# The next layer's modulation in feed forward: weighted row sums on VectorE in place of products on TensorE

## The reference, cut to what matters

```python
silu_c = jax.nn.silu(c)
silu_cc = jax.nn.silu(c_ctx)
for l in range(DEPTH):
    mod = silu_c @ ada_w[l] + ada_b[l]
    modc = silu_cc @ ada_w[l] + ada_b[l]
    sh1, sc1, g1, sh2, sc2, g2 = [m[:, None, :] for m in jnp.split(mod, 6, axis=-1)]
    ...
    h = h + g1 * y
    h = h + g2 * swiglu(modulate(h, norm2_g[l], sh2, sc2), ffn_w_in[l], ffn_w_out[l])

def swiglu(h, w_in, w_out):
    g, u = jnp.split(h @ w_in, 2, axis=-1)
    return (jax.nn.silu(g) * u) @ w_out
```

## Time and profile before

| | |
|---|---|
| median of 3 runs | 4071.4 us (4070.13 to 4071.9) |
| span of the profiled execution | 4078.4 us |
| mean granted clock of TensorE | 0.952 |
| TensorE busy | 3830.4 us (94%) |
| VectorE busy | 1355.6 us (33%) |
| ScalarE busy | 1249.7 us (31%) |
| GpSimd busy | 1260.6 us (31%) |
| DMA | 342.84 MB, mean 84 GB/s |

### The profile page before, as it was taken

One profiled execution on the slowest core, in us unless ns is written; L12 is line 12 of the kernel. 1 busy time (PEld: TensorE's weight loads), 2 busy tenths in 40 slices (PEclk: granted clock), 3 DMA queues, 4 the chain that ended last, 5 costly groups with the idle time before them and its releaser, 6 DMA issues. The chain is left out here.

```text
span 4078.4 us, 77356 instructions
## 1 busy us (share of the span) xinstructions
PE 3830.4 (94%) x32782; PEld 3174.4 (78%) x32782; DVE 1355.6 (33%) x2689; ACT 1249.7 (31%) x2182; POOL 1260.6 (31%) x658
## 2 busy tenths in 40 slices
PE   6998999999999999989799999989999989989997
PEld 5877788888777677768698888768888868667785
DVE  3345211111444211166557765251111140543111
ACT  3234311112346322232234443232111142643222
POOL 2201222222334343432234432122322223634442
PEclk7999999999999999999879989999999989999998
DMA  4223232232200434333201100133233212012221
GB/s 174 68 97 108 88 119 87 102 110 88 79 5 32 155 134 164 131 111 110 83 21 30 28 22 24 63 119 108 73 119 110 71 52 73 20 45 88 94 88 71
DMA packets 119705, 342.84 MB, mean 84 GB/s; under 512 B 34687, under 2 KB 41343, under 8 KB 119039
## 3 DMA queue, kind: packets, MB, share of 16 engines
q1 hardware_dynamic: 119423, 338.75, 24.1%
HBM read 323.89 MB, written 16.93 MB: 84 GB/s over the span
## 5 line engine op out<-in xcount | busy, mean ns | idle before, releaser
L204 POOL TENSOR_TENSOR feed_low<-ring,feed_high 128x1024 fp32r<-128x1024 f32 (+1 forms) x236 | 620.5, 2629 | 1356.2 <-ACT feed_high L197 1324.2
L221 PE MATMUL ps<-hn_high,feed_high 128*128 128x512 f32 x2016 | 720.3, 357 | 9.3 <-DVE h L1204 5.1
L221 PE MATMUL ps<-hn_low,feed_high 128*128 128x512 f32 x2016 | 714.1, 354 | 0.0
L221 PE MATMUL ps<-hn_high,feed_low 128*128 128x512 f32 x2016 | 713.3, 354 | 0.0
L221 PEld LDWEIGHTS ps<-hn_high,feed_high 128*128 128x128 f32 x2016 | 381.2, 189 | 89.8 <-issue 24.6
L221 PEld LDWEIGHTS ps<-hn_high,feed_low 128*128 128x128 f32 x2016 | 381.0, 189 | 53.7
L221 PEld LDWEIGHTS ps<-hn_low,feed_high 128*128 128x128 f32 x2016 | 381.3, 189 | 51.5
L1379 DVE TENSOR_TENSOR ps<-feed_gate,ps 128x768 f32<-128x768 f32 (+1 forms) x88 | 73.0, 829 | 1004.4 <-PE ps L221 985.4
L197 ACT ACTIVATE feed_high<-ring 128x1024 fp32r<-128x1024 f32 (+1 forms) x240 | 272.7, 1138 | 369.5 <-PE ps L221 369.4
L221 PE MATMUL ps<-feed_hid_high,feed_high 128*128 128x512 f32 (+1 forms) x1056 | 380.2, 360 | 0.0
L221 PE MATMUL ps<-feed_hid_high,feed_low 128*128 128x512 f32 (+1 forms) x1056 | 376.8, 357 | 0.0
(11 more groups left out here) (592 smaller groups left out, 7491.9 us busy)
## 6 DMA issues: line engine op xcount, KB each, us to landing
feed_side_ring<-in_ada SPq DMA_DIRECT2D x144, 512.0 KB, 5.9
ring<-in_ffn_g SPq DMA_DIRECT2D x88, 512.0 KB, 3.5
ring<-in_ffn_u SPq DMA_DIRECT2D x88, 512.0 KB, 3.5
ring<-in_ffn_d SPq DMA_DIRECT2D x64, 704.0 KB, 4.1
diff_side_ring<-in_ada SPq DMA_DIRECT2D x32, 512.0 KB, 4.3
ring<-in_od_in SPq DMA_DIRECT2D x24, 512.0 KB, 3.4
ring<-in_ev_in SPq DMA_DIRECT2D x23, 512.0 KB, 4.4
ring<-in_even_in SPq DMA_DIRECT2D x20, 512.0 KB, 3.8
```

Source lines behind the costliest of these rows:

```text
L204: pool.tensor_tensor(self.low[:, j % self.slots, 0:w], feed.ring[:, slot, 0:w], self.high[:, j % self.slots, 0:w].bitcast(F32), ALU.subtra ...
L221: mm = pe.matmul(dst, weights[a], values[b], start=first and n == 0, stop=last and n == 2)
```

## The change

For the three feed forwards with side work, `SideSums` takes the place of `SideModulation`:

- VectorE reads the tiles of `ada` itself. For each block of 128 x 512 and each of the two vectors it multiplies by a scalar of its own for each partition and adds to a running sum: 16 instructions for a group (`weigh`), of which the first two only multiply. In "first" all four tiles stand behind the chunk, in "up" two tiles behind each chunk.
- TensorE sums over partitions: four products of 256 columns for a group, with a matrix of 32 columns of which the first is 1 (`add`), in the place where `turn` stood. `accumulate` is gone.
- VectorE transposes the sums in blocks of 32 x 32 and copies every 32nd column into PSUM (`take`), behind the first chunk of an iteration. `finish` now has 16 small additions instead of 2.
- `feed_side_ring` has three slots instead of four; the fourth tile of a group takes the slot of the first. A slot is freed by VectorE, not by TensorE.
- One small DMA at the head of each stage goes.

```diff
-        ("first", 1, [(s % SIDE, io[w], 0, 24 * h + s) for s in range(4)]),
-        ("up", HALF // 2, [(s % SIDE, io[w], 4, 24 * h + 4 + s) for s in range(4)]))]
+        ("first", 1, [(s % 3, io[w], 0, 24 * h + s) for s in range(4)]),
+        ("up", HALF // 2, [(s % 3, io[w], 4, 24 * h + 4 + s) for s in range(4)]))]
...
+class SideSums:
...
+    def weigh(self, dve, i, tiles):
+        side = self.k.side
+        for j in tiles:
+            slot, before, per = side.count(side.at, j)
+            dve.wait_ge(side.landed[slot], 16 * per * i + 16 * (before + 1))
+            for b in range(2):
+                c, weights = 2 * j + b, side.ring[:, slot, 512 * b:512 * b + 512]
+                for s in range(2):
+                    scalar = self.vec[:, c, s:s + 1]
+                    if c == 0:
+                        ins = dve.tensor_scalar(self.sums[:, s, :], weights, scalar, None, ALU.mult)
+                    else:
+                        ins = dve.scalar_tensor_tensor(out=self.sums[:, s, :], in0=weights, scalar=scalar, in1=self.sums[:, s, :],
+                                                       op0=ALU.mult, op1=ALU.add)
+                if b == 0:
+                    dve.drain()
+            ins.then_inc(side.used[slot], 1)
+            dve.drain()
+        if tiles[-1] == 3:
+            dve.sem_inc(self.summed, 1)
+
+    def add(self, pe, group):
+        pe.wait_ge(self.summed, group + 1)
+        if not (isinstance(group, int) and group == 0):
+            pe.wait_ge(self.acc_read, group)
+        for s in range(2):
+            for f in range(2):
+                q = 32 * (2 * s + f)
+                mm = pe.matmul(self.acc[q:q + 32, :], self.pick[:, :], self.sums[:, s, 256 * f:256 * f + 256], start=True, stop=True)
+        mm.then_inc(self.added, 1)
+
+    def take(self, dve, group):
+        dve.wait_ge(self.added, group + 1)
+        dve.transpose(self.turned[:, :], self.acc).then_inc(self.acc_read, 1)
+        dve.drain()
+        dve.tensor_copy(self.parts[:, bass.ds(8 * group, 8)], self.turned[:, :].rearrange("p (b w) -> p b w", w=32)[:, :, 0:1].rearrange("p b w -> p (b w)"))
+        dve.drain()
...
-                    if next_c and isinstance(i, int):
-                        sm.accumulate(pe, 0, 6 * h)
-                    elif next_c and p == 0:
-                        sm.turn(pe, i + 6 * h)
-                    elif next_c:
-                        sm.accumulate(pe, i, i + (6 * h + 1))
+                    if next_c and p == 0 and not isinstance(i, int):
+                        sm.add(pe, i + 6 * h)
...
                 chunk(0, 0, 0, e)
                 if next_c:
-                    sm.copy(dve, 0, 6 * h)
+                    sm.weigh(dve, 0, range(4))
                 if h == 0 and norm.kept:
                     norm.keep(dve)
                 feed.at, side.at = up, side_base + 2 * h + 1
                 with dve.Fori(0, HALF // 2) as i:
                     for p in range(2):
                         chunk(i, p, 2 * i + (p + 1), e1)
-                    if next_c:
-                        sm.copy(dve, i, i + (6 * h + 1))
+                        if next_c and p == 0:
+                            sm.take(dve, i + 6 * h)
+                        if next_c:
+                            sm.weigh(dve, i, range(2 * p, 2 * p + 2))
```

## The result

The changed kernel takes **4124.0 us** (median of 4 runs, 4119.9 to 4127.6), the kernel before beside it 4071.7 (4070.1 to 4074.9): ratio 1.0119, 95% interval 1.0100 to 1.0138. It is slower by 52 us; 4106 (4050 to 4155) was forecast.

A forecast was written before the change was run, and what follows sets the result against it. TensorE, busy 94%, was taken as the bound. Terms of +57.0 us at 512 tokens, -31.8 and +4.5 at 768, and +5 for `finish` gave +34.7 on 4071.4: 4106 us, range 4050 to 4155.

The forecast's parts named there:

- TensorE, -2.32 us for a group: Side work of 2.87 us a group gives way to 0.55 us of `add`; over 36 groups -83.5 us if nothing else waits.
- VectorE's weighings: A group's 16 instructions take 0.46 us for the first two and 0.73 for the other 14: 11.1 us, plus GpSimd collisions.
- The first chunk of a half: VectorE weighs all four tiles there, delaying the next multiplication; at 512 tokens the second iteration starts 7.5 us later.
- The chain at 512 tokens: From slot 0's release through the `ring` tile's issue, landing, rounding and subtracting to TensorE's start: a 4.75 us pause each iteration.
- The step "0.53 us later": Within the 512-token chain, SyncE issues the next iteration's first `ring` tile 0.53 us after the fourth side tile.
- The clock, 1.7 us for a pause: TensorE's clock falling around each 512-token pause costs 1.7 us more, making an iteration 29.0 us, +4.2 us.
- 768 tokens: The same chain stays hidden by 0.45 us, an iteration gains 2.3 us; -10.6 us a half, three times -31.8.
- `keep`: In the third feed forward's first half, its 9.05 + 6.29 us follow the weighings; second iteration 12.7 us later, half +4.5 us.
- `finish`: At a stage's end, 16 instructions of 0.16 us each replace two; the stage ends 1.7 us later, three times, 5 us.
- A: Rival: the saving comes through, the side slot holding `ring` back less; complete 3993 us, in part 4060 us; chance 0.18.
- B: Rival: a wash, the two halves of the sum cancelling within 8 us, 4071 us; chance 0.09.
- C: Rival: VectorE becomes the bound through GpSimd collisions, waits and drains; +40, 4146 us; chance 0.2, within slower.

The follow-up runs named there:

- experiment 2: Changed kernel with the fourth side tile issued behind the next iteration's four `ring` tiles and 14 of a group's 16 weighings left out: 4012.8 us, ratio 0.9828.
- experiment 8: Changed kernel with the fourth side tile issued behind the `ring` tiles and running sums held in two PSUM banks at 512 tokens: 4030.4 us, ratio 0.9871.
- experiment 1: Changed kernel with only SyncE's order altered, the fourth side tile issued behind the next iteration's four `ring` tiles: 4070.6 us, ratio 0.9972.
- experiment 9: Changed kernel in its own issue order, with four side slots instead of three in the 512-token feed forward: 4087.7 us, ratio 1.0029.
- experiment 7: Changed kernel in its own issue order with three slots, 14 of a group's 16 weighings left out: 4072.7 us, ratio 0.9998.
- experiment 6: Changed kernel in its own issue order, all 16 weighings taking their third operand from PSUM, sums not formed: 4094.1 us, ratio 1.0045.
- experiment 3: Changed kernel with the fourth side tile issued behind the `ring` tiles and all 16 weighings adding zeros from PSUM, sums not formed: 4019.6 us, ratio 0.985.

## Why the prediction was right, and where it was off

The direction and the cause were right: a 4.75 us pause was forecast in each iteration at 512 tokens in front of L221, hidden at 768 tokens. The size was short, +34.7 against +41.9 between the profiled executions and +52 between the medians. In the sum of the range, the clock at 3.3 us for a pause makes (3.3 - 1.7) x 10 = +16 us and not the +8 written there, which belongs to 2.5 us; the bounds don't hang on it. By its steps:

- **TensorE, -2.32 us for a group.** 2.1 to 2.2 in experiment 2. `add` is 0.64 us for its 8 passes, where 0.55 with the wait was taken.
- **VectorE's weighings.** 11.1 us for a group and a collision more: behind the first chunk of the third feed forward they end at 2759.1, M + 18.5 to the tenth of the forecast (rows below). The single durations hold too: 0.47 us and 0.74 us were the shortest of the two kinds (0.46 and 0.73 forecast).
- **The first chunk of a half.** At 512 tokens TensorE was to begin the second iteration at M + 34.6, and began at M + 34.5 in the first half and M + 33.9 in the second.
- **The chain at 512 tokens.** Slot 0 free at M + 7.0 (forecast 7.25), `ring` tile issued M + 8.1 (7.95), TensorE starts M + 16.1 (16.0), pause 4.58 (4.75). The step "0.53 us later" was 0.88. The earlier trace rows had that already: the fourth side tile went out at 1416.31 + 3 x 0.53 = 1417.90 and the `ring` tile at 1418.77. The earlier slot made up for it, so the 0.1 us is in part luck. The pauses of the other iterations were not all like this one.
- **The clock, 1.7 us for a pause.** Here a term was mis-sized. The iteration above has 24.32 - 22.6 = 1.7 us of it, but the stage as a whole has 24 us (experiment 8) where ten times 1.7 was taken. That alone is 7 us, more than the 4 us that the stage is off: +62.8 instead of +58.7 us (57.0 and a share of `finish`). The pauses themselves vary too, and iterations run from 27.2 to 31.0, on average 29.8 against a forecast of 29.0. The page "TensorE: Matmul & The Clock Gate" of the Trainium skill, Part 1, was right that no pause of this size is free.
- **768 tokens.** Iterations of 34.5 on average against 34.0: the margin of 0.45 us was real but thin, and some pauses of about 1 us get through. -15.6 instead of -19.5 us in the first feed forward. With the late fourth tile (experiment 1) they are 34.1.
- **`keep`.** The next multiplication was to come at M + 34.5 and came at M + 30.9. From M = 2740.59:

```profile
2743.59 3.02 DVE L354 TENSOR_SCALAR feed_side_sums<-feed_side_ring,feed_mod_vec 128x512 f32<-128x512 f32 x2
2746.68 12.41 DVE L356 SCALAR_TENSOR_TENSOR feed_side_sums<-feed_side_ring,feed_mod_vec,feed_side_sums 128x512 f32<-128x512 f32 x14
2759.23 7.52 DVE L1009 SCALAR_TENSOR_TENSOR h<-h,feed_kept,feed_kept_root 128x768 f32<-128x768 f32 x8
2766.83 4.33 DVE L1015 TENSOR_SCALAR h<-h,feed_kept 128x768 f32<-128x768 f32 x8
2771.51 0.96 DVE L1432 TENSOR_TENSOR ps<-feed_gate,ps 128x768 f32<-128x768 f32 x1 [0.35 <-issue]
```

  `keep` took 11.9 us instead of the 15.3 of the earlier trace rows, which is 3.4 of the 3.6 us. In the kernel before, two of GpSimd's operations run beside it (from 2700.73 and from 2710.02); here none runs between 2754.9 and 2774.4, and the weighings in front of it have met them. I had carried a duration over together with its collision. The stage came out at -3.4 us against -4.4: what `keep` gave, the iterations behind it took.
- **`finish`.** 16 instructions in 3.06 us against 0.31: +2.75, where 1.7 was taken.

**The rivals.** A, the saving comes through, needs another order of issue: experiments 1, 2 and 8 made it happen and set its price. B, a wash: no. C, VectorE becomes the bound: not in the change (14.7 us in front of `add`), but it is what comes next when the pauses go, 31.4 us in experiment 1, 39.0 in 9. The Trainium skill ("SBUF — State Buffer", SBUF: two separate sides) has the shared port as a lock that whoever starts first holds, and the traces agree for both engines: in experiment 9 GpSimd's operation took 2.90 us instead of 2.39 when a weighing had begun 0.11 us before it, and VectorE's four weighings 5.04 us instead of 2.9.

What stays open: why the `ring` tile behind a side tile took 3.9 us from issue to ScalarE's start in one iteration (experiment 7) and 5.3 in another (experiment 6), and with it why eight of the ten pauses at 512 tokens vary between 4.6 and 6.2 us. (The other two, 3.35 and 1.75 us, follow the waits in front of `add`, behind which the granted clock was 0.68 in 1370 to 1374 and 0.50 in 1601.8 to 1606, so that TensorE itself was late.) The four-slot version at 768 tokens wasn't tried, since the ring doesn't fit there. To move `keep` out of the first chunk's way was not tried on the chip: its operand lies in memory that the hidden layer takes over.

## What to carry to other kernels

When a buffer's reader moves to another engine, look at what is queued behind the wait for its release, on the engine that issues the transfers: here four weight tiles stood behind one side tile, and moving that one tile in the list was worth some 60 us (from a ratio of 1.0119 to one of 0.9972). Follow one slot from its last reader to the next use of what waits behind it, in microseconds from a fixed event; such a chain came out to 0.1 us here in one iteration, with two errors of some 0.3 us that cancelled, and within 1.7 us in the nine others, while the shares of busy time (VectorE 46%) said nothing. Then put VectorE's running sum into PSUM where a bank is free, so that GpSimd's and VectorE's work can run beside each other.

## What the runs showed of the hardware that was not expected

- One operand in PSUM took the weighings out of GpSimd's way altogether, and cost nothing. Durations of one weighing (shortest, median, longest, in ns), first of the change, then of experiment 3:

```profile
L356 DVE SCALAR_TENSOR_TENSOR feed_side_sums<-feed_side_ring,feed_mod_vec,feed_side_sums x504: 737/750/3727, 488.0 to 3224.2; 128x512 f32<-128x512 f32 x168
```

```profile
L359 DVE SCALAR_TENSOR_TENSOR feed_side_sums<-feed_side_ring,feed_mod_vec,ps x576: 737/746/750, 478.2 to 3121.7; 128x512 f32<-128x512 f32 x192
```

  The undisturbed duration is the same, and the tail up to 3.7 us is gone, with the first operand still in SBUF.
- For a TENSOR_SCALAR it is a trade. In experiment 8:

```profile
L359 DVE TENSOR_SCALAR feed_side_sums<-feed_side_ring,feed_mod_vec x48: 471/1382/2626, 479.6 to 3116.4; 128x512 f32<-128x512 f32 x48
L359 DVE TENSOR_SCALAR ps<-feed_side_ring,feed_mod_vec x24: 744/750/756, 1345.7 to 1646.1; 128x512 f32<-128x512 f32 x24
```

  From SBUF to SBUF the shortest took 471 ns, but the median, beside GpSimd, 1382; into PSUM each took 750.
- A pause of 2.7 us was enough for the clock to fall. In experiment 7, in stretches of 1 us behind the pause that ended at 1397.51:

```profile
1396.00:1397.00 1.00, 0.00 (x0) 0.00 (x0) 0.51 (x1) 0.96 (x2) 1.00 (x1) 1.00 1.04 426
1397.00:1398.00 1.00, 0.49 (x1) 0.44 (x2) 0.64 (x4) 0.43 (x1) 0.95 (x2) 0.80 0.63 258
1398.00:1399.00 1.00, 1.00 (x4) 0.77 (x3) 0.15 (x1) 0.00 (x0) 1.00 (x1) 0.50 0.09 37
...
1401.00:1402.00 1.00, 1.00 (x6) 0.80 (x5) 0.00 (x0) 0.00 (x0) 0.00 (x0) 0.99 1.07 434
```

  Here the full clock is still granted in the pause, the fall comes when work has just begun again, and the full clock is back at 1401. (In the change the clock fell at 1415.8, 0.3 us before the work began at 1416.06.) TensorE's work in this iteration took 24.47 us instead of 22.60, so the fall cost 1.9 us; behind the pause of 4.58 us in the change it was 1.7. By stages, TensorE is busy 390.4 us in experiment 7 and 369.9 in experiment 2, 20.5 us for ten pauses of 2.7 to 4.5 us, against the change's 24 us for ten of 1.8 to 6.2 and two in front of `add`. So the clock's part hardly shrank with the pause. Behind three pauses of 1.2 to 1.5 us in experiment 9 (ending at 1394.49, 1413.14 and 1420.18) the granted clock stayed at 1.00. In this kernel, cutting a pause from 4.6 to 2.7 us left the clock's price whole.
